# Query/key and gate tiles as seven block products each, with weight sums on VectorE and a third weight buffer

## The reference, cut

```python
h = rmsnorm(x, norm1_g[l]) * (1.0 + sc1[:, None, :]) + sh1[:, None, :]
proj = h @ w_in[l]                     # (256, 1024) @ (1024, 5120)
q_m, k_m, v_m, q_d, k_d, v_d, gate_m, gate_d = jnp.split(proj, IN_SPLITS, axis=-1)
# rotary embedding of q and k; 8 + 8 attention heads of 64; two projections y_m, y_d
merged = jax.nn.sigmoid(gate_m) * y_m + jax.nn.sigmoid(gate_d) * y_d
x = x + g1[:, None, :] * (merged @ w_out[l])
h2 = rmsnorm(x, norm2_g[l]) * (1.0 + sc2[:, None, :]) + sh2[:, None, :]
y_ffn = hierarchical_moe(h2, ...)      # top 2 of 32 experts, each 1024 -> 512 -> 1024
```

## Time and profile before

| | us |
|---|---|
| Median of 3 runs (lowest, highest) | 1346.85 (1345.8, 1349.13) |
| The profiled execution | 1348.95 |
| its span (first to last instruction) | 1347.1 |
| TensorE busy | 1319.4 |
| VectorE busy | 637.0 |
| ScalarE busy | 270.8 |

### The profile page before, as it was taken

The page is one execution under the profiler, slowest core; times in us unless marked ns, Lnnn a source line. Parts: engine busy times, 40 slices in busy tenths (PEclk is TensorE's granted clock), DMA queues, the critical chain, the costliest instruction groups (busy, mean ns, idle before and its releaser), DMA issues.

```text
span 1347.1 us, 18147 instructions
## 1 busy us (share of the span) xinstructions
PE 1319.4 (98%) x6910; PEld 918.0 (68%) x6910; DVE 637.0 (47%) x1384; ACT 270.8 (20%) x566; POOL 58.9 (4%) x60
## 2 busy tenths in 40 slices
PE   9999999999999999999899999999999999999997
PEld 6888888888899888888685788854333433443332
DVE  4652389998426776720531455244333333332322
ACT  2311133220203000100442431033111111112112
POOL 0002112000000111100000000000000000000001
PEclk9999999999999999999999999999999999999999
DMA  7345333343447988767553344569999999999995
GB/s 270 126 153 160 108 126 127 126 141 125 167 146 267 323 300 308 228 192 262 226 181 131 126 188 168 207 227 414 419 423 427 427 428 428 427 427 428 425 422 218
DMA packets 122219, 350.93 MB, mean 261 GB/s; under 512 B 4768, under 2 KB 66464, under 8 KB 108704
## 3 DMA queue, kind: packets, MB, share of 16 engines
q1 hardware_dynamic: 120528, 348.68, 67.9%
q10 hardware_dynamic: 1616, 1.20, 0.3%
HBM read 348.82 MB, written 1.05 MB: 260 GB/s over the span
## 4 chain that ended last, share of the span: by engine, by line
PE 82%; DMA 7%; DVE 6%; issue 2%; ACT 1%; DVEq 1%; POOLq 0%; POOL 0%; SPq 0%; ACTq 0%
PE bank L769 38%; PE bank L1216 20%; PE bank L1019 6%; DMA arena<-in_w_gate 4%; PE bank L1096 4%; PE bank L1188 3%; PE bank L1306 2%; DVE arena L1881 2%; DMA dense<-in_w_gate 2%; PE bank L1034 2%; DVE scratch L1895 1%; PE bank L983 1%; PE bank L971 1%; PE bank L1048 1%; PE bank L822 0%
## 5 line engine op out<-in xcount | busy, mean ns | idle before, releaser
L769 PE MATMUL bank<-hT,dense 128*128 128x256 f32 x2048 | 446.0, 380 | 1.3 <-ACT hT L1407 0.8
L769 PEld LDWEIGHTS bank<-hT,dense 128*128 128x128 f32 x2048 | 388.5, 190 | 57.7 <-issue 6.3
L1216 PE MATMUL bank<-arena,scratch 128*64 128x512 f32 x864 | 228.0, 599 | 6.1 <-DMA arena<-in_w_gate 5.7
L1216 PEld LDWEIGHTS bank<-arena,scratch 128*64 128x64 f32 x864 | 71.0, 138 | 130.6 <-issue 118.5
L769 PE MATMUL bank<-arena,dense 128*128 128x256 f32 x704 | 154.6, 381 | 0.4 <-DVE arena L1957 0.4
L769 PEld LDWEIGHTS bank<-arena,dense 128*128 128x128 f32 x704 | 134.4, 191 | 20.1 <-issue 2.0
L1881 DVE SCALAR_TENSOR_TENSOR arena<-arena,par 128x256 f32<-128x256 f32 x240 | 97.8, 485 | 0.0
L2349 DVE TENSOR_TENSOR scratch<-scratch,bank 128x512 f32<-128x512 f32 x64 | 41.2, 684 | 92.1 <-PE bank L1306 90.7
L1216 PE MATMUL bank<-arena,hT 128*64 128x512 f32 x336 | 78.0, 596 | 0.7 <-ACT hT L1667 0.7
L1019 PE MATMUL bank<-region,dense 128*128 128x256 f32 x352 | 76.1, 379 | 0.0
L1019 PEld LDWEIGHTS bank<-region,dense 128*128 128x128 f32 x352 | 67.0, 190 | 9.0
(11 more groups left out here) (355 smaller groups left out, 1173.9 us busy)
## 6 DMA issues: line engine op xcount, KB each, us to landing
dense<-in_w_in SPq DMA_DIRECT2D x23, 2048.0 KB, 8.2
arena<-in_w_gate SPq DMA_DIRECT2D x21, 2048.0 KB, 22.4
arena<-in_w_up SPq DMA_DIRECT2D x20, 2048.0 KB, 22.4
arena<-in_w_down SPq DMA_DIRECT2D x17, 2048.0 KB, 24.7
arena<-in_w_ada SPq DMA_DIRECT2D x12, 2048.0 KB, 8.1
dense<-in_w_ffn_up SPq DMA_DIRECT2D x22, 1024.0 KB, 7.7
dense<-in_w_down SPq DMA_DIRECT2D x8, 2048.0 KB, 28.9
arena<-in_w_up SPq DMA_DIRECT2D x14, 1024.0 KB, 23.7
```

The lines of the kernel that those rows point to most:

```text
L769: last = mm(dst, chunk(k, m), src[:, k, :], start=k == 0, stop=k == k_n - 1)
L1216: last = mm(dst[e * CAP:(e + 1) * CAP, :], tokens(k, e), w[e][:, k, :], start=k == 0, stop=k == k_n - 1)
```

## The change

Each query/key tile and each gate tile becomes seven block products (the Winograd form of Strassen's scheme). The tile is seen as two by two: two groups of output channels by two groups of 128 tokens, and the 1024 input channels are two halves of four chunks. A block product is four matmuls of 128 x 128 weights with 128 columns. Weight sums (four additions of 128 x 512 per tile, `weight_sums`) and four sums of hT (`token_sums`) are made by VectorE. The products of a tile come in three blocks, `first` (16 matmuls), `second` (8) and `third` (4), in an order that runs over tiles (`fast_order`). After `first`, ScalarE copies two products out of the bank and VectorE adds (`fix_first`), after `second` it adds once (`fix_second`), after `third` it completes the four quarters in the bank (`fix_third`), and only then ScalarE reads the tile.

The units of this stretch go through three buffers, the third being `expert[6]`. The sums lie in `expert[0]` and `expert[1]`, so the first two gate matrices and the down matrix that goes to `expert[6]` are loaded after the last gate tile. The first query/key unit is loaded after the second down unit. Three semaphores are merged into others without moving anything.

```diff
+def buffer(n):
+    if FAST0 <= n < FAST1:
+        return (2, FAST0 % 2, 1 - FAST0 % 2)[(n - FAST0) % 3]
+    return n % 2
+SLOTS = {"p1": 0, "p3": 1, "p6": 2, "p5": 3, "p7": 2, "p2": 0, "p4": 2}
+BLOCK = {"first": ("p1", "p3", "p5", "p6"), "second": ("p7", "p2"), "third": ("p4",)}
+def fast_order():
+    out = [("first", 0)]
+    for t in range(NFAST):
+        if t + 1 < NFAST:
+            out.append(("first", t + 1))
+        out.append(("second", t))
+        if t:
+            out.append(("third", t - 1))
+    return out + [("third", NFAST - 1)]
...
@@ SyncE
+                if u == 1:
+                    load("qk", 0, flat, wi2[:, :, 0:512])
-            for e in range(2):
-                load_matrix("gate", e, 0)
+            load("qk", 1, flat, wi2[:, :, 512:1024])
+            load("qk", 2, flat, wi2[:, :, 1536:2048])
             sp.wait_ge(sem_("ada_summed"), 48)
             for e in range(2):
                 load_matrix("up", e, 0)
...
+            sp.wait_ge(tile_done, TILE["gate2", 7] + 1)
+            for e in range(2):
+                load_matrix("gate", e, 0)
             load_matrix("down", 1, 0)
...
@@ TensorE
-            for u in range(4):
-                unit_512("qk", u, hT, ready=None if u else by_chunk("r1_out"))
+            fast("qk", 0, "first", 0, 8, ready=first_tokens)
+            fast("qk", 1, "first", 0, 8)
+            fast("qk", 0, "first", 8, 16, ready=first_tokens)
+            fast("qk", 1, "first", 8, 16)
+            for block, t in ORDER[2:]:
+                fast("qk", t, block)
...
-                some(0, 6)
-                attend(a, lambda: some(6, KD))
+                some(14 * a, 14 * a + 10)
+                attend(a, lambda: some(14 * a + 10, 14 * a + 14))
@@ ScalarE
+            for t in range(NFAST):
+                copy_products("qk", t)
+                if t >= 3:
+                    read_qk(t - 3)
...
+                elif a and a % 2 == 0:
+                    copy_products("gate2", a // 2)
+                    if a >= 6:
+                        read_gate2((a - 6) // 2)
@@ VectorE
+            for t in range(NFAST):
+                if t == 0:
+                    weight_sums("qk", 2)
+                fix_first("qk", t)
+                if t:
+                    fix_second("qk", t - 1)
+                    if t >= 2:
+                        fix_third("qk", t - 2)
+                    if t + 2 < NFAST:
+                        weight_sums("qk", t + 2)
+                if t == 1:
+                    unscale()
+                if t >= 4:
+                    rope(t - 4)
...
+            SUM_STEPS = {3: (4, (0, 1)), 4: (4, (2, 3)), 5: (5, (0, 1)), 6: (5, (2, 3)), 9: (6, (0, 1)), 10: (6, (2, 3)),
+                         11: (7, (0, 1)), 12: (7, (2, 3))}
...
+                elif a % 2:
+                    fix_second("gate2", a // 2 - 1)
+                    if a >= 5:
+                        fix_third("gate2", a // 2 - 2)
+                if a in SUM_STEPS:
+                    weight_sums("gate2", *SUM_STEPS[a])
```

More of the change, by code:

```diff
@@ L159, in program @@
         up_slot, down_slot = [expert[2], expert[3]], [expert[4], expert[5]]
+        bufs = [dense[0][:], dense[1][:], expert[6]]
+        sum_sets = [[v3(arena[:, (3 * i + q) * 512:(3 * i + q + 1) * 512], P) for q in range(3)] for i in range(4)]
+        token_sums = [v3(arena[:, 6144 + 512 * q:6144 + 512 * (q + 1)], P) for q in range(4)]
         wdt = sb("wdt", KD * H)
@@ L313, in program @@
         x_in = [sem(f"x_in{c}") for c in range(TT)]
-        dense_in = [sem(f"dense_in{s}") for s in range(2)]
+        dense_in = [sem(f"dense_in{s}") for s in range(3)]
         gate_in, up_in, down_in = ([sem(f"{n}_in{r}") for r in range(2)] for n in ("gate", "up", "down"))
@@ L374, in arrived @@
         def arrived(n):
-            names = [k for m in range(n % 2, n + 1, 2) for k, (u, c) in UNIT.items() if u <= m < u + c]
+            names = [k for m in range(n + 1) if buffer(m) == buffer(n) for k, (u, c) in UNIT.items() if u <= m < u + c]
             return sum(32 if k in HALVES else 16 for k in names)
@@ L789, in unit_halves, with fast, raw @@
                          None if j else ready)
+            def fast(name, t, block, i0=0, i1=None, ready=None):
+                b = v3(bank[TILE[name, t] % NB][:], P)
+                w = v3(bufs[buffer(U0(name) + t // 2)], 512)
+                s1, s2, s4 = sum_sets[t % 4]
+                t1, t2, t3, t4 = token_sums
+                products = BLOCK[block]
+                for i in range(i0, 4 * len(products) if i1 is None else i1):
+                    p, k = products[i // 4], i % 4
+                    if (block, i) == ("first", 0):
+                        open_tile(name, t)
+                        pe.wait_ge(sem_("sums_ready"), sums_count(name, t))
+                    if block == "second" and i == 0:
+                        pe.wait_ge(sem_("fast_fixed"), fast_count(name, "first", t))
+                    if block == "third" and i == 0:
+                        pe.wait_ge(sem_("fast_fixed"), fast_count(name, "second", t))
+                    if block == "first" and ready is not None:
+                        ready(p, k)
+                    def raw(h, m):
+                        o = (2 * (t % 2) + m) * P
+                        return w[:, 4 * h + k, o:o + P]
+                    left, right = {
+                        "p1": (raw(0, 0), hT[:, k, TOK[0]]), "p2": (raw(1, 0), hT[:, 4 + k, TOK[0]]),
+                        "p3": (s4[:, k, :], hT[:, 4 + k, TOK[1]]), "p4": (raw(1, 1), t4[:, k, :]),
+                        "p5": (s1[:, k, :], t1[:, k, :]), "p6": (s2[:, k, :], t2[:, k, :]),
+                        "p7": (raw(0, 1), t3[:, k, :])}[p]
+                    last = mm(b[:, SLOTS[p], :], left, right, start=k == 0, stop=k == 3)
+                    if i == 4 * len(products) - 1:
+                        last.then_inc(tile_done if block == "third" else sem_("fast_part"), 1)
             def stage(name, units, unit, src):
@@ L2173, in _, with rope @@
             cos, sin = bc(con("cos"), 2), bc(con("sin"), 2)
-            for t in range(8):
+            def rope(t):
                 dst = qk[:, 2 * t:2 * t + 2, :]
```

179 lines of the change are left out of this document (139 added, 40 removed).

## The result

The changed kernel took 1354.63 us, the median of five runs (1353.81 to 1357.09), against 1348.86 for the kernel before (five runs beside it, 1345.8 to 1349.13). Ratio 1.0054, 95% interval 1.0038 to 1.007. (The ratio is taken over all executions, whose means are 1355.15 and 1347.91; the two medians differ by only 5.8 us.) The forecast was 1354.4, a rise of 7.6 on a median of 1346.85. That the medians agree to 0.2 us is partly luck: the rise was smaller and the kernel before slower than assumed. So the sign is sure, and the size is 0.4 to 0.9%.

A forecast was written before the change was run, and what follows sets the result against it. TensorE was taken as the bound up to the first expert product, transfers after it. Down stage with clock 5.3, query/key 0.5, attention 1.8 and moved loads 0 gave +7.6 us: 1354.4 for the median, range 1346 to 1361.

The forecast's parts named there:

- Prices: TensorE's products: 0.4335 us with 256 columns, 0.2233 with 128; 0.68 us less per tile, 10.9 us in all.
- Rival 5: Narrow products on TensorE are bound by their weight loads: 0.38 us each, +61 us, 1416; chance 0.02.
- Down stage, +3.5 for the wait: Down stage: TensorE waits 3.5 us for the third down load, queued behind the first query/key load.
- Rival 1: Down stage: the queue lets the down load through or it is hidden, no wait; 1349.1, no change; chance 0.20.
- The clock behind it, +1.8: Behind the down load's wait: a lower granted clock costs 1.8 us more.
- Query/key, +0.5: Query/key stage: saving 5.5 us against waits for chunks, token sums, bank reads and the last fix-up; +0.5 us.
- Attention, +1.8: Attention and gates: saving 5.5 us against 2.4 of small waits and 4.9 for gate tiles 6 and 7; +1.8 us.
- Rival 2: VectorE and ScalarE stay ahead of TensorE, so all 10.9 us arrives except the down wait; 1341.2, faster; chance 0.08.
- Moved expert loads, 0, and one for one behind: Expert loads moved after the last gate tile cost 0; each microsecond before 896.40 moves the end by one.
- Rival 4: The output weights are late behind the moved loads: +5.1 us, 1359.5; chance 0.05.
- Rival 3: Clock also falls at sums waits (2 x 1.7 us), or VectorE's bank reads cost more; 1357.8 to 1361; chance 0.20.
- the likeliest case: Whole kernel: the forecast's own sum, 1354.4 us, alone 1351 to 1359; chance 0.45.

The follow-up runs named there:

- late first unit: The changed kernel with the first query/key unit loaded behind the third down load instead of ahead of it; 1351.22 us, ratio 1.0027.
- gates alone: Block products for gate tiles only, query/key tiles wide as in the kernel before, first query/key unit loaded behind the third down load; 1350.17 us, ratio 1.0012.
- loads alone: Only the loads of the change, with all arithmetic of the kernel before (wide products, no sums); 1355.88 us, ratio 1.0065.
- sums nearly free: The changed kernel with each weight sum made for 8 of its 128 columns only, so the output is not the reference's; 1353.34 us, ratio 1.0038.
- The loads alone with a late first unit: Loads of the change with arithmetic of the kernel before, first query/key unit loaded behind the third down load; 1347.52 us, ratio 0.9996.
- second comparison of the changed kernel: The changed kernel run once more, unaltered, against the kernel before; 1358.25 us, ratio 1.0074.
- seven edits of order: The changed kernel with a load, weight sums, ScalarE's reads and copies and a rotation reordered, the work unchanged; 1343.93 us, ratio 0.997.
- the sums together: The changed kernel with all four weight sums of gate tile 6 at head 9 and of tile 7 at head 11; 1355.17 us, ratio 1.0057.

## Why the prediction was right, step by step

**Prices: right.** In the rows below eight records (four products) follow each other every 0.89 us, 0.223 for a product. Rival 5 is out, and so is its milder form, the 0.32 estimated from the Trainium skill (TensorE: Matmul & The Clock Gate, Back-to-back issue gap): the measured 0.223 decides.

**Down stage, +3.5 for the wait: right.** 3.7 and 3.9 us on the changed kernel, near 584 as forecast, and gone when the query/key load stands behind the down load. The queue works in order here: the third down load took 13.1 us to land, 7.7 before. Rival 1 is out. The Trainium skill (DMA: Bandwidth & Descriptors, Two DMAs through the same engine are not ordered) says that nothing orders transfers across the 16 engines; no run here shows one transfer overtaking another by it.

**The clock behind it, +1.8: right on the mean (1.7), wrong for the first profile (0),** and too small for the comparisons: the load in front costs 3.6 or 6.3 us by the changed kernel with it and without it (1.0054 and 1.0074 against 1.0027), and 9 with wide products, where 5.3 was forecast. The stretch from the end of the down stage to the first query/key product took 17.67 us in the first profile and 19.36 in the second (648.04 to 667.40), but that fall can't be laid to the down wait: it is in two of the seven with this wait and in three of the seven without it. What all executions show is their mean clock: 0.9925 to 0.9950 in the seven runs with the wait, 0.9954 to 0.9967 in the others. Only one execution of each run has a profile, so where the others lose their time isn't shown.

**Query/key, +0.5: measured +1.6** (and 2.0 between the late first unit and the gates alone, 1.0027 and 1.0012). Each wait was found and sized by its recorded length: 4 x 0.8 forecast, 4 x 0.86 measured; 0.8 and 0.67 for the last block. What the forecast had wrong is the price of a wait: it costs more than its record. The timeline of TensorE in the changed kernel, one tile with its wait:

```profile
697.80 1.06 PE L889 MATMUL bank<-arena,dense 128*128 128x128 f32 x8
698.69 1.06 PE L889 MATMUL bank<-hT,dense 128*128 128x128 f32 x8
699.58 1.06 PE L889 MATMUL bank<-arena,dense 128*128 128x128 f32 x8
701.50 2.05 PE L889 MATMUL bank<-hT,arena 128*128 128x128 f32 x16 [0.86 <-ACT region L1690]
```

Eight records take 0.89 us while others follow and 1.06 where nothing does; behind the wait the first products are another 0.1 late. From wait to wait a tile takes 701.50 - 694.12 = 7.38 us where 28 x 0.223 = 6.25: 1.13 for a wait of 0.86. Five waits at 0.27 more are 1.35. The start (chunks, token sums) cost 20.42 - 84 x 0.223 = 1.7 of the 1.9 forecast. In all -5.5 + 1.7 + 4 x 1.13 + 0.94 = +1.6.

**Attention, +1.8: the sum came out at +1.6 by luck, with two errors that cancel.** The places and the cause of the two waits are right: without a fall between them they are 2.0 and 2.0 (gates alone) where 2.4 to 2.5 each was forecast. Part of the difference is a slip: the terms listed for VectorE add up to 9.2, not 9.35, and the trace has 8.95 from the end of the scores to the first product that needs the sums (791.09 to 800.04). In the changed kernel they took only 3.1 (2.0 and 1.1), not 4.9, because a clock fall of 1.7 us between them (0.86 in 800 to 812) gives VectorE time. The prediction foresaw this shortening and charged nothing for such a fall; but the second wait became only 0.95 shorter, so 0.75 of the 1.7 was not paid out of it. Waits and clock together make 4.8 (3.1 + 1.7), which looks like the forecast 4.9. From the first scores to the end of the two projections the gates alone take 109.3 us and the loads alone 107.05, 2.25 more, of which 1.7 is the clock. Rival 2 is out: with sums nearly free the helpers do stay ahead, and even then 1.7 of the 5.5 us doesn't come.

**Not foreseen: the fall in the profile of before.** The earlier trace rows has the clock at 0.83 in 816 to 822. The prediction read it as a sign of what a wait costs, not as 1.7 us that this execution had already paid and the next might not pay. In the changed kernel the same work (sums of squares, the two projections) took 0.8 and 0.9 us less, and this hid the fall at head 10 in the balance: 3.8 + 1.6 + 1.6 (scores to last values) - 1.7 = 5.3, the shift of the first expert product, where 7.6 was forecast: 5.3 for the down stage, 0.5, 1.8 and nothing. The errors in the terms (in this profile +1.8 for the clock that didn't fall behind the down wait, -1.1 in query/key, 1.7 for the profile of before) partly cancel. The forecast 7.6 is 0.56%, inside the 0.4 to 0.9% of the two comparisons.

**Moved expert loads, 0, and one for one behind: right.** The loads alone with a late first unit are at 0.9996. Over fourteen profiles the gathering of tokens ahead of the first expert product begins between 888 and 903 us, and the program ends 453.5 to 456.7 us later. Rival 4 is out. Rival 3 (waits cost more than they last, 1357.8 to 1361) names part of what the second comparison of the changed kernel shows, by its median of 1358.25; the two comparisons lie on both sides of the border between it and the likeliest case. Of its mechanism, the fall behind the first sums wait is shown; that VectorE's reads of a bank under way cost more is not.

## What to carry to other kernels

Fewer columns on the bound engine are worth only what the helpers' queues let through: 10.9 us of products were saved here by the prices, and seven edits of order, which change no work, turned +0.5 to +0.7% into -0.3%. When a wait is removed, ask what stands behind it in each helper's queue before counting the gain; the sums together gave nothing until ScalarE's bank read was moved too. Put a load that is not urgent behind one that TensorE will wait for, even if its buffer has been free for long; here that alone was worth 3.6 to 9 us.

## What the hardware showed unexpectedly

One kernel, with the same waits to 0.2 us, had a span of 1352.0 and of 1356.2 us. Of the difference, 2.85 us lie in the 264 records behind the down wait and 1.7 in the normalizations, both with a granted clock below 1. Some places have a fall in one profile and none in the next, others have it nearly always: behind this wait of about 4 us it came in six of seven profiles and cost 1.5 to 2.9 us; behind the sums wait of 2.0 us at head 10 it came in four of five, and in the fifth (gates alone) behind the same wait at head 12; in the normalizations (waits of 1.9 and 0.9 us) in five of fourteen, and behind the wait before the sums of squares (1.6 to 1.9 us) in the profile of before only. These shorter waits' falls cost about 1.7 us each. A microsecond taken off the recorded down wait gave back 1.1 us of time in one comparison (3.6 / 3.2), 1.9 in another (6.3 / 3.3) and 2.4 with wide products (9.3 / 3.9); so one comparison can be off by 2.7 us from the next for a kernel with such waits. Most of this spread goes with the clock: the mean over the executions was 0.9950 in the first comparison of the changed kernel, 0.9925 in the second and 0.9954 with the late first unit; in proportion to 1350 us, an estimate, the clock accounts for 0.5 us in the first and 3.9 in the second, beside waits that are 3.2 and 3.3 us longer. Together that is 3.7 and 7.2, where the ratios give 3.6 and 6.3.
